# Which engine subtracts: the low parts of the weight chunks of units 0 to 11, and a softplus in three steps

## What is computed

```python
h = rms_norm(x, norm_mix_g)
u = h @ w_in                      # 2048 x 12352: q | k | v | z | conv stream x, B, C | dt
attn = merge of three dilated-window attentions over q, k, v          # 16 heads of 128
xbc = silu(conv(xbc, conv_w) + conv_b)                                # 5 taps
dt = softplus(dt_raw + dt_bias);  A = -exp(a_log)
y = ssd(x*dt, dt*A, B, C) forward + the same backward + x * d_skip    # 8 groups of 4 heads
ssd = rms_norm(y * silu(z), norm_g)                                   # per group
x = x + concat(attn, ssd) @ w_out                                     # 4096 x 2048
x = x + relu(rms_norm(x, norm_mlp_g) @ w_up)^2 @ w_down               # 2048 x 8192 x 2048
```

## Time and profile before

| | us |
|---|---|
| profiled execution, span from the first to the last instruction | 1661.57 |
| TensorE busy, of the span | 1547.4 (93%) |
| VectorE busy | 781.7 (47%) |
| ScalarE busy | 726.7 (44%) |
| GpSimd busy | 956.1 (58%) |

### The profile page before, as it was taken

How to read it: one execution, slowest core, us unless ns; L and a number is a source line. 1 busy time by engine, 2 the same in 40 slices (tenths; PEclk the granted TensorE clock), 3 DMA queues, 4 the chain that set the end, 5 groups by cost and what they waited for, 6 DMA issues and landing times.

```text
span 1661.6 us, 26094 instructions
## 1 busy us (share of the span) xinstructions
PE 1547.4 (93%) x9501; PEld 1383.6 (83%) x9501; DVE 781.7 (47%) x1169; ACT 726.7 (44%) x851; POOL 956.1 (58%) x413
## 2 busy tenths in 40 slices
PE   5898778787699999999999999999999999999998
PEld 5797678776577888888888999889988999889987
DVE  5799899889986646464412322111221121112211
ACT  4253445433454455454434444334443444334442
POOL 4364355343454666565566566666666656666664
PEclk9999889888899999999999999999999999999999
DMA  8664545354445656656555665666656665566563
GB/s 254 189 200 143 149 125 166 102 153 154 125 151 152 185 174 174 190 169 230 180 192 179 176 191 183 196 194 183 182 195 189 178 188 189 191 189 179 179 200 103
DMA packets 186335, 291.58 MB, mean 175 GB/s; under 512 B 13533, under 2 KB 67151, under 8 KB 185984
## 3 DMA queue, kind: packets, MB, share of 16 engines
q1 hardware_dynamic: 183748, 285.92, 56.7%
q10 hardware_dynamic: 2492, 4.36, 0.9%
HBM read 288.04 MB, written 5.34 MB: 177 GB/s over the span
## 4 chain that ended last, share of the span: by engine, by line
PE 79%; DVE 12%; issue 7%; DVEq 1%; DMA 1%; ACT 0%; POOL 0%; ACTq 0%
PE psum L1170 78%; DVE mix L795 3%; DVE mix L804 2%; DVE conv L820 1%; DVE conv L824 1%; DVE cbm L835 1%; DMA x_in<-in_x 1%; DVE actT_lo L771 1%; PE psum L1269 0%; PE psum L1289 0%; DVE w_lo L777 0%; DVE dt_p L1026 0%; PE psum L1215 0%; DVE xbc L829 0%; DVEq L795 0%
## 5 line engine op out<-in xcount | busy, mean ns | idle before, releaser
L430 POOL TENSOR_TENSOR w_lo<-raw,w_hi 128x1024 fp32r<-128x1024 f32 x384 | 939.3, 2451 | 675.5 <-ACT w_hi L492 674.6
L492 ACT ACTIVATE w_hi<-raw 128x1024 fp32r<-128x1024 f32 x512 | 540.7, 1059 | 789.9 <-PE psum L1170 789.9
L1170 PE MATMUL psum<-actT_lo,w_hi 128*128 128x256 f32 x1792 | 517.9, 289 | 17.5 <-DVE w_lo L777 12.1
L1170 PE MATMUL psum<-actT_hi,w_lo 128*128 128x256 f32 x1792 | 512.9, 286 | 0.0
L1170 PE MATMUL psum<-actT_hi,w_hi 128*128 128x256 f32 x1792 | 512.3, 286 | 0.0
L1170 PEld LDWEIGHTS psum<-actT_lo,w_hi 128*128 128x128 f32 x1792 | 350.2, 195 | 28.3 <-DVE w_lo L777 12.9
L777 DVE TENSOR_TENSOR w_lo<-raw,w_hi 128x1024 fp32r<-128x1024 f32 x128 | 161.3, 1260 | 440.2 <-ACT w_hi L492 438.1
L1170 PEld LDWEIGHTS psum<-actT_hi,w_lo 128*128 128x128 f32 x1792 | 350.4, 196 | 0.2
L1170 PEld LDWEIGHTS psum<-actT_hi,w_hi 128*128 128x128 f32 x1792 | 350.0, 195 | 0.0
L1170 PE MATMUL psum<-w_hi,hid_lo 128*128 128x512 f32 x512 | 199.2, 389 | 0.0
L1170 PE MATMUL psum<-w_lo,hid_hi 128*128 128x512 f32 x512 | 199.2, 389 | 0.0
(11 more groups left out here) (189 smaller groups left out, 1464.3 us busy)
## 6 DMA issues: line engine op xcount, KB each, us to landing
raw<-in_w_in SPq DMA_DIRECT2D x128, 512.0 KB
raw<-in_w_up SPq DMA_DIRECT2D x128, 512.0 KB
raw<-in_w_down SPq DMA_DIRECT2D x128, 512.0 KB
raw<-in_w_out SPq DMA_DIRECT2D x64, 512.0 KB
raw<-in_w_in SPq DMA_DIRECT2D x64, 256.0 KB
raw<-in_w_in SPq DMA_DIRECT2D x128, 128.0 KB
decay<-decay_rows SPq DMA_DIRECT2D x16, 512.0 KB, 5.7
rel_tiles<-rel_rows ACTq DMA_DIRECT2D x1, 3072.0 KB, 15.0
```

What stands on the lines that cost most here:

```text
L430: pool.tensor_tensor(w_lo[i][:, :, :], raw[j][:, :, :], w_hi[i][:, :, :].bitcast(f32), ALU.subtract).then_inc(lo_pool, 1)
L492: act.activation(w_hi[j % RING][:, :, :], raw[j][:, :, :], ACT.Copy).then_inc(hi_ready, 1)
L1170: return pe.matmul(o, lhsT, rhs, start=first, stop=last, **kw)
```

## The change

All low parts of units 0 to 11, and of the first three chunks of unit 12 (they are made three slots ahead, in window 3), go to VectorE; GpSimd's loops over these units are gone. From there on the split of six to two is as before. The waits count `lo_dve` alone for the early chunks, and with a base for the later ones. At the start VectorE makes the low part of chunk R-1 behind `x_low(R-1)`, and that of chunk 7 behind `x_low(7)`. The softplus steps go in three parts to slots 6, 7 and 8; scans, store, transposes and copy of the token parameters move one slot later.

```diff
+EARLY = 12
-        def wait_low(eng, U, j):
-            if j in DVE_CHUNKS:
-                eng.wait_ge(lo_dve, len(DVE_CHUNKS) * U + DVE_CHUNKS.index(j) + 1)
+        def is_early(U, j):
+            return CH * U + j < CH * EARLY + LEAD
+
+        def wait_low(eng, U, j, early=False):
+            if early or (isinstance(U, int) and is_early(U, j)):
+                eng.wait_ge(lo_dve, CH * U + j + 1)
+            elif j in DVE_CHUNKS:
+                base = CH * EARLY + LEAD - len(DVE_CHUNKS) * EARLY
+                eng.wait_ge(lo_dve, len(DVE_CHUNKS) * U + (base + DVE_CHUNKS.index(j) + 1))
             else:
-                eng.wait_ge(lo_pool, len(POOL_CHUNKS) * U + POOL_CHUNKS.index(j) + 1)
+                base = len(POOL_CHUNKS) * EARLY + LEAD
+                eng.wait_ge(lo_pool, len(POOL_CHUNKS) * U + (POOL_CHUNKS.index(j) + 1 - base))
...
@@ GpSimd
-                    if j in POOL_CHUNKS:
+                    if j in POOL_CHUNKS and not (isinstance(a, int) and is_early(12 + 3 * a + r, j)):
                         low(12 + 3 * a + r, j)
...
-            for U in range(3):
-                unit(U)
-            with pool.Fori(3, 12) as U:
-                unit(U)
@@ ScalarE: store of the scans
-                if s == 11:
+                if s == 12:
@@ VectorE
-            def low_ahead(U0, s):
+            def low_ahead(U0, s, early=False):
                 n, j = divmod(s + LEAD, CH)
-                if j in DVE_CHUNKS:
+                if early or j in DVE_CHUNKS:
                     low(U0 + n, j)
...
                 x_gain_root(R)
                 if R > 0:
                     x_low(R - 1)
-                if R == 3:
-                    low(0, 3)
+                    low(0, R - 1)
+            x_low(7)
             low(0, 7)
-            x_low(7)
...
-            def dt_softplus():
+            def dt_softplus(part):
+                if part == 2:
+                    ...  # the seven polynomial steps (15, 13, ... 3)
+                if part == 3:
+                    ...  # last product, max, sum, times A
...
-                low_ahead(0, s)
-                if s == 6:
-                    dt_softplus()
-                if s == 8:
+                low_ahead(0, s, True)
+                if 6 <= s < 9:
+                    dt_softplus(s - 5)
+                if s == 9:
                     dt_sums()
-                if s == 13:
+                if s == 14:
                     dt_tokens()
...
             def ssd_window(w, m):
                 for s in range(WIN):
-                    low_ahead(3 * w, s)
+                    low_ahead(3 * w, s, True)
                     ssd_slot(s, m)
@@ TensorE: transposes of the token parameters
-                if s == 12:
+                if s == 13:
```

More of the change, by code:

```diff
@@ L288, in _, with load @@
         def _(sp):
-            def load(U, j, pieces):
+            def load(U, j, pieces, early=False):
                 if positive(U):
-                    wait_low(sp, U - 1, j)
+                    wait_low(sp, U - 1, j, early)
                 at = 0
@@ L309, in ssd_window @@
                         load(3 * w + r, j, [in_cols(j, COL_X + 256 * g, 256), in_cols(j, COL_B + 128 * g, 128),
-                                            in_cols(j, COL_C + 128 * g, 128)])
+                                            in_cols(j, COL_C + 128 * g, 128)], True)
                         if m is None and s == 5:
@@ L316, in ssd_window @@
                     else:
-                        load(3 * w + r, j, [in_cols(j, COL_Z + UNIT * w)])
+                        load(3 * w + r, j, [in_cols(j, COL_Z + UNIT * w)], True)
                     decay_loads(s, w, m)
@@ L1012, in then_step @@
                 dve.wait_ge(dt_step, step[0])
-            def dt_softplus():
+            def dt_softplus(part):
+                if part == 2:
+                    for k in (15, 13, 11, 9, 7, 5, 3):
+                        then_step(stt_(p, p, 1.0 / k, z2, ALU.add, ALU.mult))
+                    return
+                if part == 3:
+                    then_step(stt_(p, p, 1.0, z, ALU.add, ALU.mult))
+                    then_step(ts_(r, v, 0.0, None, ALU.max))
+                    then_step(stt_(soft_dt, p, 2.0, r, ALU.mult, ALU.add))
+                    then_step(ts_(a_dt, soft_dt, dtcol[:, 4:5], None, ALU.mult))
+                    return
                 dve.wait_ge(dt_done, 1)
@@ L1024, in dt_softplus @@
                 then_step(ts_(p, z2, 1.0 / 17, None, ALU.mult))
[L1025 to L1030, removed]
             def dt_sums():
@@ L1172, in _, with chunk_by_weights @@
             pe.sem_inc(y_done, PER_GROUP)
-            def chunk_by_weights(U, j, pair, skip=False):
-                wait_low(pe, U, j)
+            def chunk_by_weights(U, j, pair, early=False):
+                wait_low(pe, U, j, early)
                 i = j % RING
@@ L1331, in _ @@
                     pe.wait_ge(xl_ready, j + 1)
-                chunk_by_weights(r, j, r)
+                chunk_by_weights(r, j, r, True)
                 if s + 3 < CH:
@@ L1355, in ssd_window @@
                             pe.wait_ge(z_ready, w)
-                    chunk_by_weights(3 * w + r, j, r)
+                    chunk_by_weights(3 * w + r, j, r, True)
                     ssd_slot(s, m)
```

## The result

The changed kernel takes 1595.8 us (median of 4 runs, 1594.24 to 1597.04), the kernel before 1663.42 beside it: a ratio of 0.9594, 95% interval 0.958 to 0.9607. The forecast was 1596. The profiled execution has a span of 1595.30 us, 66.3 less than before.

The account below looks back on a forecast made before the run. VectorE was taken to bound before 432 us, TensorE from 502 us. Span 1661.57 - 53.1 (windows 1 to 3) - 15.0 (window 0) = 1593.5, plus 1.2 for the runs' median and 1 for moved steps: 1596 us; 8-in-10 range 1586 to 1613.

Parts of the forecast that it names:

- (a): SSD windows 1 to 3: GpSimd's 54 low parts vanish and with them VectorE's stalls, 104.3 us less.
- Rival C: The long times are VectorE's own, so stalls stay and added low parts cost: 1735 us, chance 0.04.
- (b): SSD windows 1 to 3: 54 more low parts on VectorE, 1.14 us each, add 61.6 us.
- (c): Windows 1 to 3: VectorE's 13.4 us wait before low parts goes; 3.0 us of group_norm waits for ScalarE come.
- (d): Window 0, first chunks: TensorE's waits for rs_diag, actT_lo and dt_lo shrink, 5.0 us less (bounds 0 and 6.1).
- (f): Window 0, slots 12 to 23: VectorE keeps up and starts window 1 less far behind TensorE, 2.2 us less.
- (e): Window 0: softplus in three parts ends TensorE's stand and half clock around chunk 11, 7.8 us less (lower bound 3.5).
- (g): Window 0: the moved scans, store, transposes and parameter copy cost 0, at most 2 us; 1 us was added.
- the later stages: Attention window from 432.18 us and all behind it keep 69.9 and 1159.5 us, plus or minus 3 us.
- A: Lockstep: VectorE waits on every high part, 2.3 us a group, and 5 us of window 0 is lost: 1612 us, chance 0.15.
- B: Window 0 gives only its lower bound, 3.5 us, for instance through shared DMA engines: 1607 us, chance 0.13.
- D: More gain: no new wait, the full 17 us in window 0, 3 us in the attention window: 1587 us, chance 0.12.

Follow-up runs that it names:

- Run 5: The changed kernel, but the 54 added low parts in windows 1 to 3 subtract only 8 of 512 columns: 1566.54 us (0.9422).
- Run 7: The changed kernel with VectorE's loop over windows 1 to 3 written out: 1589.67 us (0.9561).
- run 1: The changed kernel, but with the softplus in one piece in slot 6 and the steps behind it in their old slots: 1599.73 us (0.9619).
- run 2: The kernel before, with only the softplus spread over slots 6 to 8 and the steps behind it one slot later: 1658.93 us (0.9977).
- run 3: The changed kernel plus 54 GpSimd subtractions of a constant tile from itself in windows 1 to 3, result unused: 1675.67 us (1.008).

## Why the prediction was right, step by step

**(a) The stalls.** Right, and shown by the two runs with GpSimd back, not only by the coincidence of ends in the earlier trace rows. The sum was 104.3 us. Measured: VectorE's busy time in the stage, in which overlaps count once, fell by 40.0 us (286.73 to 246.73) although 54 more low parts of 1.14 us were in it: 40.0 + 61.6 = 101.6. The 61.6 in it is counted and not measured by itself; the groups of instructions, taken one by one, give 100. One term was too large: I had 376 ns for an undisturbed scaling, from the shortest and the middle one, and it is 412 (479 and 345 by shape), so its excess is 96 x (526 - 412) = 10.9 us and not 14.4. Rival C falls: with GpSimd away no first tap is over 0.5 us.

**(b) The price.** 61.6 us, at 1.14 each. The stage's low parts have a mean of 1220 ns and no stalls. Run 5 takes nearly all of it away and gets 29.3 us, since TensorE then binds; that they lie on the path up to that point is shown, the rest of the 61.6 is only counted.

**(c) The waits.** The total was right (262.4 for 263.09 us), its parts were not. What VectorE was not busy fell from 28.7 to 16.4 us (315.45 - 286.73, 263.09 - 246.73), 12.4 less where I had 10.4. No instruction of group_norm waits for Ln and Exp: the 3.0 us did not come. (The bound of 2.3 us that I gave for such a wait was the mean of five waits and not the longest, which is 3.1.) Small waits for masks, norms and means went that I had not counted. And of the 13.4 us before low parts that I let go, 5.7 stayed. 5.0 of these are marked "issue": the turn of VectorE's loop, twice. In the trace of before one of the two turns was put down as "issue" (2.1) and the other as a wait for ScalarE; neither was removable by this change. Run 7 shows what they are, with 6.1 us for writing the loop out. TensorE stands less than I foresaw, 19 us for mixing matrices and sq_lo (11.8 + 7.2) where I had 25 for the former alone; that it does not bind, and that its clock passes 0.95 (it is 0.99), held.

**(d), (f) The start.** The first instructions of window 1 come at 102.80 (forecast 102). Of (d) the timeline of the start shows each part:

```profile
13.55 0.48 DVE L745 TENSOR_SCALAR rs_diag<-ident,small 128x128 f32<-128x128 f32 x2 [0.45 <-POOL small L433]
...
39.76 0.68 DVE L775 TENSOR_TENSOR actT_lo<-xg,actT_hi 128x512 fp32r<-128x512 f32 x1
...
44.77 1.23 DVE L1004 TENSOR_TENSOR dt_lo<-dt_raw,dt_hi 128x1024 fp32r<-128x1024 f32 x1
...
58.07 3.11 DVE L1020 SCALAR_TENSOR_TENSOR dt_p<-dt_p,dt_z 64x256 f32<-64x256 f32 x7
```

rs_diag takes 0.48 us for 2.55, actT_lo 0.68 for a mean of 1.72, and dt_lo starts at 44.77 where it started at 49.14: 4.4 us of the 5.0. The seven polynomial steps take 3.11 us (3.2 forecast). Of the 13.9 us that window 0 gives, 4.4 for (d) and the 7.8 of (e) leave 1.7 for (f), where I had 2.2.

**(e) The softplus.** Here the place in the sum was wrong, though not the sum. TensorE's 7.8 us do go (from 52 to 117 us it is busy 65.00 of 65.00 us, at a clock of 1.00), but 3.9 of them by the absence of GpSimd alone, as run 1 against the changed kernel shows; the spread alone takes 3.5 (run 2). Whoever had made only this edit on the forecast's word would have got half.

**(g), SyncE, the later stages.** The moved steps cost nothing that shows: no wait of VectorE for the copied parameters, none of TensorE for weight loads at a DMA share of 0.59 (0.58 forecast) in windows 1 to 3 and 0.84 in window 0. The last two stages kept their lengths to 0.1 us; the 3 us allowed for another phase were not needed.

**The rivals.** A: VectorE waits 0.4 us for high parts in the whole stage, not 14. B: window 0 gives 13.9 us, not 3.5. D: it was right on the waits for ScalarE, but the turns of the loop took their place.

## What to carry to other kernels

An engine that is near its limit can get faster by taking work back from the engine that it excludes: here 54 subtractions on VectorE cost it 62 us and rid it of 102 us of standing. Compare the shortest and the median time of one instruction form before believing a busy share; where they are apart by one instruction of another engine, that engine's work is the price. Move the border between the two to where the other bound takes over (here the end of the SSD groups), and look for empty time at the turns of loops on the engine that binds.

## What the runs showed of the hardware

- What GpSimd does decides which VectorE instruction stands. Beside its subtraction, which reads SBUF, instructions with one and with two inputs from SBUF were held up: first taps with a median of 1988 ns, later taps to 2119, SiLU 2584. Beside its memsets first taps (median 2072 ns) and decay arguments (to 2073), which have one, were held up, and those with two kept their times: later taps 474 ns, SiLU 1216. The Trainium skill (SBUF — State Buffer, Who interferes with whom) says just this: two SBUF inputs contend with a GpSimd that reads, and not with one that only writes, while a two-port mode contends with either. These runs agree; that first taps and decay arguments run in such a mode is inferred, no run here shows it by itself.
- One microsecond of GpSimd's subtractions cost VectorE 0.78 us before the change (101.6 of 54 x 2.42 = 131) and the kernel 0.74 in run 3 (79.9 of 54 x 2.00 = 108). Here 2.42 and 2.00 us are the medians of GpSimd's subtraction in the two kernels; in run 3 its mean is 2.30, since GpSimd stands for VectorE as well (up to 4.9 us for one). My 90 to 130 us had gone by the longer subtraction, and at its upper end took every one as held.
- The turn of VectorE's loop over a window of about 185 instructions (556 in three) is 2.5 us in which VectorE executes nothing, twice in 263 us. The same instructions in a row have no such gap. What VectorE does in that time no run here shows.
